# Sample tokens' gathered dots moved into the U products, and six ring slots for the V products

## The chip, the cores and the metric

The kernel runs on one core of one Trainium2 chip. The metric is the device time of one execution in microseconds (us). Five engines work side by side, each on its own instruction list: TensorE (PE, matrix products), VectorE (DVE), ScalarE (ACT), GpSimd (POOL) and SyncE (SP, which here only issues loads). They meet through semaphores.

## The reference, cut to what matters

One inference step of a hybrid decoder of two layers, for 256 prompt tokens and 32 sample tokens (8 sequences of 4), model width 1024. Each layer has a mixer and then a block of single-neuron experts (PEER), and only the latter is touched:

```python
def peer(h, wq, k1, k2, u, v):        # 16384 experts, 8 heads, top 16 each
    ...
    q = (xb @ wq).reshape(-1, PEER_HEADS, 2, half)
    s1 = jnp.einsum('thd,nd->thn', q[:, :, 0], k1)
    s2 = jnp.einsum('thd,nd->thn', q[:, :, 1], k2)
    ...                                # top 16 of 128 + 128 keys, then of their sums
    act = jax.nn.gelu(jnp.einsum('thkd,td->thk', jnp.take(u, idx, axis=0), xb).astype(jnp.float32))
    return jnp.einsum('thk,thkd->td', (gw * act).astype(xb.dtype), jnp.take(v, idx, axis=0))
```

So a token needs, for each of its 128 chosen experts, the dot product with a row of u, its GELU, a gate weight, and then the weighted sum of the rows of v.

## The kernel before

The 256 prompt tokens are computed densely: all 16384 experts, as 128 tiles of 128, each tile 128 x 1024 floats (512 KB). `experts_block` makes the **U products** (tile of u times tokens, GELU, into `m.act`), `gates_block` multiplies `m.act` by the gates of the chosen experts, and `combine_block` makes the **V products** (tile of v times `m.act`, summed over all tiles in PSUM as `ps_y`). The host lays all tiles of a layer out in the order of use in one array, `stream`; SP loads them in order into a ring of `RING` = 3 slots (`load_many`), each load waiting until the slot's tile of three before is done.

A float32 tile is multiplied in two parts. ACT copies a half tile (128 x 512) to a rounded high part (`split_high`, line 393), another engine subtracts it from the tile to make the low part (`split_low`, line 400), and PE multiplies high with high, high with low and low with high parts: 24 matmuls of 256 columns a tile (lines 443 and 447 in U, 2444 and 2448 in V). `parts` has three buffers of half a tile. The subtraction of the second half frees the ring slot (`m.done`). In U the first `TOPK_TILES` = 51 tiles have both subtractions on GpSimd, because DVE is searching the top experts; from there GpSimd has the first half and DVE the second. In V, DVE has both, and GpSimd makes the low part of the activations (line 2493, `act_parts`, once a tile). `each_tile` runs such a body over a range of tiles in loops of one **turn**, three tiles.

The 32 sample tokens are not computed densely. Their 32 x 128 choices are laid over the 128 partitions, 32 to a partition (`SLOTS` = 32), and one **gather** (an indirect DMA issued by GpSimd, line 2501) fetches one row of 1024 floats for each partition, 512 KB together, into one of the two buffers `m.rows`. All of this stands in `combine_block`: from turn `DOT` = 1, 16 turns (`HALF`) with two gathers from `u_rows` and two dot products on DVE each (`tile_dot`, line 2530: one instruction multiplies and sums a row buffer with `m.tokens`); then ACT's GELU of the 32 sums (line 2479), which waits for the last dot, and the product with the weights; then, from turn `ADD` = 18, 16 turns with two gathers of rows of v and two weighted additions into `m.tokens` each (`tile_add`, line 2542). GpSimd issues the next fetch of a buffer when DVE has counted the buffer used (`row_used0`, `row_used1`). Late in the stage PE sums the four partitions of each token (`samples_ready`, `ps_m`, line 2455).

Of the kernel before, what the change touches and what calls it, by code (L numbers as in the profile page):

```python
# [30 lines left out]
DEPTH = 2  # L31
NP = 256
# [178 lines left out]
class Memory:  # L211


    def __init__(self, nc, ctx):
# [65 lines left out]
        self.picks = t.take(NP // SPOTS * HEADS * TOPK // 2).bitcast(BF16)  # L280
        self.spots = self.rows.rearrange("p a b -> p (a b)").bitcast(BF16)
# [131 lines left out]
def each_tile(eng, first, end, body):  # L413

    assert first % RING == 0
    start, turns = first // RING, end // RING
    if turns - start == 1:
        for j in range(RING):
            body(start, j)
    elif turns > start:  # L420
        with eng.Fori(start, turns) as g:
            for j in range(RING):
                body(g, j)
    for n in range(turns * RING, end):
        body(turns, n % RING)
# [1629 lines left out]
def experts_block(nc, m, l, hr, stream, spots_in):  # L2055
# [3 lines left out]
             "picked exp_ready gates_ready turned picks_ready spots_loaded")  # L2059
    SCORES1, SCORES2, TOKENS = 2 * RING, 9 * RING, 10 * RING  # L2060
    SOFT, TURNED = TOPK_TILES + 3 * RING, TOPK_TILES + 6 * RING
    GROUPS = ((HEADS, 0, m.sel[:, :, 0, :]), (HEADS, 1, m.sel[:, :, 1, :]), (HEADS // FOLD, 0, m.sel[:, :, 2, 0:SLOTS]))
    with signals(nc, names) as s, nc.psum_tensor("ps_s", [P, 4, 512], F32) as ps_s, \
# [60 lines left out]
        def _(act):  # L2124
# [50 lines left out]
            each_tile(act, TURNED + RING, NKEYS - 2, tile)  # L2175
# [4 lines left out]
        def _(pool):  # L2180
# [6 lines left out]

            each_tile(pool, 0, TOPK_TILES, tile)
            each_tile(pool, TOPK_TILES, NKEYS, first_half)

        @block.vector
        def _(v):
# [110 lines left out]
            each_tile(v, SOFT + 2 * RING, NKEYS, second_half)  # L2303
# [99 lines left out]
def combine_block(nc, m, l, stream, u_rows):  # L2403

    AHEAD = 3
    assert RING % AHEAD == 0 and PARTS == 3
    TURNS = NKEYS // RING
    HALF = SLOTS // 2
    DOT, ADD = 1, 2 + HALF
    assert ADD + HALF <= TURNS - 3  # L2410
    names = ("step zeroed summed hi_ready lo_ready parts_used act_hi act_lo x_ready squares_ready sums_ready root_loaded "
             "root_ready row_used0 row_used1 dots_ready act_ready weighted samples_ready samples_summed")
    with signals(nc, names) as s, nc.psum_tensor("ps_y", [P, KD, NP], F32) as ps, \
            nc.psum_tensor("ps_n", [P, 512], F32) as ps_n, nc.psum_tensor("ps_m", [P, 512], F32) as ps_m, \
            nc.sbuf_tensor("act_parts", [P, AHEAD, 2, NP], F32R) as act_parts, \
            nc.sbuf_tensor("zeros", [P, 512], BF16) as zeros, \
            nc.sbuf_tensor("gated", [P, KD, NSAMP], F32) as tmp, nc.Block() as block:

        def column(g, j):
            return m.act[:, ds(g * RING + j, 1), :].squeeze(1)  # L2420
# [351 lines left out]
```

## Time and profile before

| | |
|---|---|
| median of 3 runs | 2501.21 us (2496.72 to 2512.55) |
| profiled execution | 2507.76 us, span 2506.0 us |
| PE, PEld busy | 2313.6 us (92%), 2094.0 us (84%) |
| DVE, ACT, GpSimd busy | 1556.4, 1240.3, 1081.1 us |
| DMA | 455.45 MB, mean 182 GB/s |
| granted PE clock, mean | 0.947 |

The span is the time from the first to the last instruction of the profiled execution; the rest of its time lies around it. A busy share is a mean over stages with different limits. PEld is the loading of weights, beside the matmuls. A row of a group gives the source line, engine, operation, the operands and how many; then busy time and mean time of one; then the idle time of the engine just before them and who ended it. In the view in order of time a row begins with start and duration, and ends with the idle time before it and its releaser.

### The profile page before, as it was taken

The page shows a single profiled execution, that of the slowest core. Times are in us where ns is not written, and L with a number is a line of the kernel's source. Part 1 is how long each engine was busy: PE and PEld are TensorE (multiplying, and loading weights), DVE is VectorE, ACT ScalarE, POOL GpSimd, SP SyncE. Part 2 cuts the span into 40 slices and gives each one's busy share as a digit, 9 for nine tenths or more (in the row PEclk, how much of TensorE's full clock was granted, in tenths as well). Part 3 has the DMA queues.
Part 4 walks back from the last instruction along what each step waited for, and adds up shares of the span by engine and source line. Part 5 has one row for each costly group of instructions (what it writes and reads, how often), then busy time and mean ns, then how long its engine had stood idle before and what let it go on. Part 6 is the DMA issues. An engine that isn't in the chain of part 4 may idle for free. (4 is left out here: it accounts for less than half of the span.)

```text
span 2506.0 us, 59086 instructions
## 1 busy us (share of the span) xinstructions
PE 2313.6 (92%) x20464; PEld 2094.0 (84%) x20484; DVE 1556.4 (62%) x3131; ACT 1240.3 (49%) x2355; POOL 1081.1 (43%) x1000
## 2 busy tenths in 40 slices
PE   5967999999999999999979679999999999999998
PEld 4933777999998799999969248699999988999997
DVE  3466634993224987888554766359632278888875
ACT  3530113557556955555545302145675587555554
POOL 0005202884445755555200141058744476555641
PEclk8966899999999999999989689999999999999999
DMA  6556123555553088888544560345555512888873
GB/s 263 165 176 211 53 87 126 177 179 198 186 190 111 0 270 286 280 288 279 178 147 159 185 219 3 111 160 177 184 201 188 189 43 93 281 294 273 287 244 129
DMA packets 123813, 455.45 MB, mean 182 GB/s; under 512 B 13744, under 2 KB 14256, under 8 KB 122544
## 3 DMA queue, kind: packets, MB, share of 16 engines
q1 hardware_dynamic: 105264, 386.80, 44.5%
q0 software_dynamic: 18432, 67.12, 10.0%
q8 instruction: 71, 1.16, 0.2%
q14 instruction: 46, 0.38, 0.0%
HBM read 449.37 MB, written 4.49 MB: 181 GB/s over the span
## 5 line engine op out<-in xcount | busy, mean ns | idle before, releaser
L393 ACT ACTIVATE parts<-ring 128x512 fp32r<-128x512 f32 x1128 | 698.9, 629 | 534.9 <-PE ps_u L447 281.7
L400 DVE TENSOR_TENSOR parts<-ring,parts 128x512 fp32r<-128x512 f32 x770 | 594.5, 796 | 510.3 <-ACT parts L393 488.7
L400 POOL TENSOR_TENSOR parts<-ring,parts 128x512 fp32r<-128x512 f32 x358 | 463.9, 1298 | 475.6 <-ACT parts L393 460.8
L2444 PE MATMUL ps_y<-act_parts,parts 128*128 128x256 f32 x4096 | 566.7, 280 | 11.4 <-ACT parts L393 11.0
L443 PE MATMUL ps_u<-h_parts,parts 128*128 128x256 f32 x4096 | 563.5, 280 | 0.9 <-ACT parts L393 0.6
L2444 PEld LDWEIGHTS ps_y<-act_parts,parts 128*128 128x128 f32 x4096 | 516.1, 188 | 17.3 <-ACT parts L393 16.8
L443 PEld LDWEIGHTS ps_u<-h_parts,parts 128*128 128x128 f32 x4096 | 514.9, 188 | 3.4 <-ACT parts L393 1.9
L2493 POOL TENSOR_TENSOR act_parts<-big,act_parts 128x256 fp32r<-128x256 f32 x256 | 235.8, 921 | 242.5 <-ACT act_parts L2473 239.9
L2448 PE MATMUL ps_y<-act_parts,parts 128*128 128x256 f32 x2048 | 328.9, 282 | 7.5 <-DVE parts L400 5.9
L447 PE MATMUL ps_u<-h_parts,parts 128*128 128x256 f32 x2048 | 322.3, 279 | 1.4 <-DVE parts L400 1.1
L2448 PEld LDWEIGHTS ps_y<-act_parts,parts 128*128 128x128 f32 x2048 | 275.4, 188 | 18.7 <-DVE parts L400 17.1
L447 PEld LDWEIGHTS ps_u<-h_parts,parts 128*128 128x128 f32 x2048 | 275.6, 188 | 2.2 <-DVE parts L400 1.5
L2473 ACT ACTIVATE act_parts<-big 128x256 fp32r (+1 forms) x256 | 106.7, 417 | 183.1 <-PE ps_y L2448 176.0
L2338 PEld LDWEIGHTS ps_g<-onehot 128*128 128x128 f32 x1024 | 128.4, 194 | 36.6 <-issue 31.2
L443 PE MATMUL ps_z<-x_parts,parts 128*128 128x288 f32 x832 | 132.5, 303 | 27.1 <-ACT parts L393 27.1
L2338 PE MATMUL ps_g<-onehot 128*128 128x128 f32 x1024 | 146.7, 287 | 6.5 <-ACT onehot L2370 3.4
L2358 POOL TENSOR_TENSOR onehot<-keep,sel 128x512 f32<-128x512 f32 x128 | 133.0, 1042 | 37.6 <-PE ps_g L2338 26.7
L443 PEld LDWEIGHTS ps_z<-x_parts,parts 128*128 128x128 f32 x832 | 121.0, 195 | 28.3 <-ACT parts L393 28.3
L459 PE MATMUL ps_mod<-ring,cond 128*32 128x256 f32 x768 | 78.9, 514 | 52.6 <-DMA ring<-in_stream 42.2
L2542 DVE SCALAR_TENSOR_TENSOR big<-big 128x1024 f32<-128x1024 f32 x64 | 102.5, 1602 | 29.7 <-DMA big<-in_stream,big 29.5
L2530 DVE SCALAR_TENSOR_TENSOR big<-big 128x1024 f32<-128x1024 f32 x64 | 91.7, 1432 | 39.0 <-DMA big<-in_u_rows,big 38.5
L2501 POOL DMA_INDIRECT big<-in_stream,big x64 | 76.0, 1187 | 71.9 <-DVE big L2542 68.1
(384 smaller groups left out, 2552.0 us busy)
## 6 DMA issues: line engine op xcount, KB each, us to landing
ring<-in_stream SPq DMA_DIRECT2D x696, 512.0 KB
big<-in_stream SPq DMA_DIRECT2D x16, 512.0 KB, 11.7
out_state_out<-big SPq DMA_DIRECT2D x2, 1440.0 KB, 7.0
big<-in_state SPq DMA_DIRECT2D x2, 1280.0 KB, 11.1
big<-in_mixc SPq DMA_DIRECT2D x2, 1024.0 KB, 8.5
big<-in_spots SPq DMA_DIRECT2D x2, 1024.0 KB, 5.4
x_res<-in_x SPq DMA_DIRECT2D x1, 1152.0 KB, 5.1
out_y<-big SPq DMA_DIRECT2D x4, 288.0 KB, 2.1
```

The costliest lines, as they stand in the source:

```text
L393: eng.activation(m.parts[:, q % PARTS, 0, :], half_tile(m, t, half), ACT.Copy).then_inc(s["hi_ready"], 1)
L400: eng.tensor_tensor(m.parts[:, q % PARTS, 1, :], half_tile(m, t, half), m.parts[:, q % PARTS, 0, :].bitcast(F32), ALU.subtract).then_inc(m ...
L443: pe.matmul(out, hi[:, k, :], hr[:, side, kk, 0:tokens], start=(kk + side == 0), stop=False)
L447: mm = pe.matmul(out, lo[:, k, :], hr[:, 0, kk, 0:tokens], start=False, stop=(kk == KD - 1))
L2338: mm = pe.matmul(ps_g[:, g % SETS, c, :], first[:, g % SETS, c, :], second[:, g % SETS, c, :], start=True, stop=True)
L2358: pool.tensor_tensor(second[:, g % SETS, :, :], spread(m.iota, 1, GROUP), spread(tokens_of(m.second_key, i, g), 2, P), ALU.subtract).then_ ...
L2444: pe.matmul(ps[:, half * KD // 2 + k, :], hi[:, k, :], act_parts[:, j % AHEAD, side, :], start=False, stop=False)
L2448: mm = pe.matmul(ps[:, half * KD // 2 + k, :], lo[:, k, :], act_parts[:, j % AHEAD, 0, :], start=False, stop=False)
L2473: act.activation(act_parts[:, j % AHEAD, 0, :], column(g, j), ACT.Copy).then_inc(s["act_hi"], 1)
L2493: pool.tensor_tensor(act_parts[:, j % AHEAD, 1, :], column(g, j), act_parts[:, j % AHEAD, 0, :].bitcast(F32), ALU.subtract).then_inc(s["ac ...
L2530: v.scalar_tensor_tensor(m.rows[:, q, :], m.rows[:, q, :], 1.0, m.tokens, ALU.mult, ALU.mult, accum_out=m.dot[:, ds((g - DOT) * 2 + q, 1)] ...
L2542: v.scalar_tensor_tensor(m.tokens, m.rows[:, q, :], m.dot[:, ds((g - ADD) * 2 + q, 1)], m.tokens, ALU.mult, ALU.add).then_inc(s[f"row_used ...
```

## The change

The dot products of the sample tokens move from `combine_block` to `experts_block`. There they stand in the 16 turns from `DOTS` = tile 69 to `DOTS_END` = tile 117, two gathers and two dots a turn as before, into two buffers `m.dot_rows` that lie where the activations of tiles 120 to 127 come later. GpSimd's loop is written out for these turns, and each fetch stands behind a first-half subtraction; DVE does a dot behind the second-half subtraction of the second and third tile of a turn. ACT's GELU of the sums waits at tile 120, DVE's product with the weights at tile 123.

In `combine_block` the ring has six slots (`VRING`: the three of `m.ring` and three in `more_ring`), a turn has six tiles, and the 16 turns with additions, from `ADD` = 1, have one addition behind the third and one behind the sixth tile. `act_parts` has two slots instead of three, `zeros` and `gated` move into `m.sel`, and the order of the PSUM tensors changes.

```diff
@@ Memory
+        self.dot_rows = Area(self.big, (NKEYS - 2 * D // NP) * NP).take(2, D)
@@ experts_block
+    HALF = SLOTS // 2
+    DOTS, DOTS_END = TURNED, TURNED + RING * HALF
@@ scalar
-            each_tile(act, TURNED + RING, NKEYS - 2, tile)
+            each_tile(act, TURNED + RING, DOTS_END + RING, tile)
+            act.wait_ge(s["dots_ready"], 1)
+            act.activation(m.dot, m.dot, ACT.Gelu_apprx_tanh).then_inc(s["dots_out"], 1)
+            each_tile(act, DOTS_END + RING, NKEYS - 2, tile)
@@ gpsimd
+            def fetch(n, q):
+                if n:
+                    pool.wait_ge(s[f"row_used{q}"], n)
+                pool.indirect_dma_start(m.dot_rows[:, q, :], None, u_rows,
+                                        bass.IndirectOffsetOnAxis(ap=m.u_row[:, 2 * n + q:2 * n + q + 1], axis=0)).then_inc(
+                    m.fetched[q], 16)
-            each_tile(pool, TOPK_TILES, NKEYS, first_half)
+            each_tile(pool, TOPK_TILES, DOTS - RING, first_half)
+            pool.wait_ge(s["found"], 3)
+            for turn in range(DOTS // RING - 1, DOTS_END // RING):
+                n = turn - DOTS // RING
+                for j in range(RING):
+                    first_half(turn, j)
+                    if j == 0 and n >= 0:
+                        fetch(n, 1)
+                    if j == 2 and n + 1 < HALF:
+                        fetch(n + 1, 0)
+            each_tile(pool, DOTS_END, NKEYS, first_half)
@@ vector
-            each_tile(v, SOFT + 2 * RING, NKEYS, second_half)
+            each_tile(v, SOFT + 2 * RING, DOTS, second_half)
+            def dot(g, j):
+                second_half(g, j)
+                if j:
+                    q, n = j - 1, g - DOTS // RING
+                    v.wait_ge(m.fetched[q], l * (2 * HALF * 16) + n * 16 + 16)
+                    v.scalar_tensor_tensor(m.dot_rows[:, q, :], m.dot_rows[:, q, :], 1.0, m.tokens, ALU.mult, ALU.mult,
+                                           accum_out=m.dot[:, ds(n * 2 + q, 1)]).then_inc(s[f"row_used{q}"], 1)
+            v.wait_ge(s["tokens_out"], 2)
+            each_tile(v, DOTS, DOTS_END, dot)
...
+            v.memset(m.tokens, 0.0)
+            each_tile(v, DOTS_END, DOTS_END + 2 * RING, second_half)
+            v.wait_ge(s["dots_out"], 1)
+            link(v.tensor_tensor(m.dot, m.dot, m.weight, ALU.mult))
+            each_tile(v, DOTS_END + 2 * RING, NKEYS, second_half)
@@ combine_block
-    AHEAD = 3
+    AHEAD = 2
-    TURNS = NKEYS // RING
+    TURNS = NKEYS // VRING
-    DOT, ADD = 1, 2 + HALF
+    ADD = 1
+            nc.sbuf_tensor("more_ring", [P, RING, D], F32) as more, \
+        def slot(j):
+            if j < RING:
+                n = T_V + j
+                return m.ring[:, n % RING, :], m.loaded[n % RING], m.done[n % RING], n // RING
+            return more[:, j - RING, :], s[f"loaded{j}"], s[f"done{j}"], 0
@@ sync
-            load_many(sp, m, stream, l, T_V + RING, TILES)
+            for j in range(RING, VRING):
+                tile, loaded, _, _ = slot(j)
+                sp.dma_start(tile, stream[l, T_V + j, :, :]).then_inc(loaded, 16)
+            with sp.Fori(1, TURNS) as g:
+                for j in range(VRING):
+                    load(g, j)
@@ scalar
-                act.wait_ge(s["parts_used"], g * 2 * RING + (2 * j + PARTS - 2))
+                act.wait_ge(s["parts_used"], g * 2 * VRING + (2 * j + PARTS - 2 * AHEAD + 2))
@@ gpsimd
             for turn in range(TURNS):
+                n = turn - ADD
-                for j in range(RING):
+                for j in range(VRING):
                     tile(turn, j)
+                    if j == 0 and 0 <= n < HALF:
+                        fetch(n, 1)
+                    if j == 3 and 0 <= n + 1 < HALF:
+                        fetch(n + 1, 0)
@@ vector
             def tile_add(g, j):
                 tile(g, j)
-                if j:
-                    q = j - 1
+                if j % RING == RING - 1:
+                    q, n = j // RING, g - ADD
```

## Rows read from the trace of the kernel before

**Rows 1.** The page's busy tenths, TensorE, 40 slices of 62.65 us each.

```profile
PE   5967999999999999999979679999999999999998
```

**Rows 2.** Busy time by stretch: busy and (count) per engine, clock, DMA share, GB/s.

```profile
640.00:780.00 140.00, 140.00 (x1202) 140.00 (x1201) 34.58 (x50) 76.87 (x151) 64.60 (x50) 1.00 0.58 187
883.00:1028.00 145.00, 139.10 (x1141) 134.78 (x1140) 119.57 (x157) 74.28 (x143) 84.17 (x79) 1.00 0.85 284
1038.00:1180.00 142.00, 138.44 (x1150) 135.17 (x1149) 124.87 (x125) 75.17 (x144) 80.53 (x79) 1.00 0.87 291
```

**Rows 3.** Groups of plain U products, 640 to 780 us.

```profile
L443 PE MATMUL ps_u<-h_parts,parts 128*128 128x256 f32 x802 | 109.8, 279 | 0.0
...
L400 POOL TENSOR_TENSOR parts<-ring,parts 128x512 fp32r<-128x512 f32 x50 | 64.6, 1292 | 75.4 <-ACT parts L393 75.4
...
L400 DVE TENSOR_TENSOR parts<-ring,parts 128x512 fp32r<-128x512 f32 x50 | 34.6, 692 | 105.4 <-ACT parts L393 105.4
```

**Rows 4.** Order of time in plain U products, GpSimd.

```profile
702.08 1.29 POOL L400 TENSOR_TENSOR parts<-ring,parts 128x512 fp32r<-128x512 f32 x1 [1.51 <-ACT parts L393]
```

**Rows 5.** Order of time in V, GpSimd's activation splits of tiles 3, 54, 105, both layers.

```profile
882.87 0.73 POOL L2493 TENSOR_TENSOR act_parts<-big,act_parts 128x256 fp32r<-128x256 f32 x1 [0.50 <-ACT act_parts L2473]
...
1038.42 0.74 POOL L2493 TENSOR_TENSOR act_parts<-big,act_parts 128x256 fp32r<-128x256 f32 x1 [0.68 <-ACT act_parts L2473]
...
1190.41 0.74 POOL L2493 TENSOR_TENSOR act_parts<-big,act_parts 128x256 fp32r<-128x256 f32 x1 [2.06 <-ACT act_parts L2473]
...
2114.79 0.74 POOL L2493 TENSOR_TENSOR act_parts<-big,act_parts 128x256 fp32r<-128x256 f32 x1 [0.63 <-ACT act_parts L2473]
...
2267.67 0.74 POOL L2493 TENSOR_TENSOR act_parts<-big,act_parts 128x256 fp32r<-128x256 f32 x1 [0.68 <-ACT act_parts L2473]
...
2421.19 0.74 POOL L2493 TENSOR_TENSOR act_parts<-big,act_parts 128x256 fp32r<-128x256 f32 x1 [2.09 <-ACT act_parts L2473]
```

**Rows 6.** Groups of the V stretch with dots, 883 to 1028 us.

```profile
L2444 PE MATMUL ps_y<-act_parts,parts 128*128 128x256 f32 x761 | 105.5, 280 | 4.5 <-ACT parts L393 4.4
...
L400 DVE TENSOR_TENSOR parts<-ring,parts 128x512 fp32r<-128x512 f32 x95 | 79.0, 876 | 5.4 <-ACT parts L393 5.3
L2448 PE MATMUL ps_y<-act_parts,parts 128*128 128x256 f32 x380 | 61.5, 284 | 1.4 <-DVE parts L400 1.4
L393 ACT ACTIVATE parts<-ring 128x512 fp32r<-128x512 f32 x96 | 57.7, 625 | 40.7 <-DMA ring<-in_stream 28.8 <-PE ps_y L2448 10.2 <-issue 1.5
...
L2530 DVE SCALAR_TENSOR_TENSOR big<-big 128x1024 f32<-128x1024 f32 x31 | 44.8, 1447 | 20.8 <-DMA big<-in_u_rows,big 20.6
```

**Rows 7.** Groups of the V stretch with additions, 1038 to 1180 us.

```profile
L400 DVE TENSOR_TENSOR parts<-ring,parts 128x512 fp32r<-128x512 f32 x94 | 78.3, 881 | 3.0 <-ACT parts L393 3.0
...
L393 ACT ACTIVATE parts<-ring 128x512 fp32r<-128x512 f32 x96 | 58.4, 627 | 33.8 <-DMA ring<-in_stream 18.0 <-PE ps_y L2448 12.1 <-issue 3.4
...
L2542 DVE SCALAR_TENSOR_TENSOR big<-big 128x1024 f32<-128x1024 f32 x31 | 51.4, 1659 | 14.2 <-DMA big<-in_stream,big 14.0 <-issue 0.2
```

**Rows 8.** Order of time in two turns with dots, GpSimd and DVE.

```profile
910.65 2.17 DVE L2530 SCALAR_TENSOR_TENSOR big<-big 128x1024 f32<-128x1024 f32 x1
...
913.10 1.16 POOL L2501 DMA_INDIRECT big<-in_u_rows,big  x1 [1.37 <-DVE big L2530]
...
916.27 1.66 POOL L2493 TENSOR_TENSOR act_parts<-big,act_parts 128x256 fp32r<-128x256 f32 x1 [1.24 <-ACT act_parts L2473]
...
918.07 1.23 POOL L2501 DMA_INDIRECT big<-in_u_rows,big  x1
...
919.00 1.22 DVE L2530 SCALAR_TENSOR_TENSOR big<-big 128x1024 f32<-128x1024 f32 x1
...
926.88 1.23 DVE L2530 SCALAR_TENSOR_TENSOR big<-big 128x1024 f32<-128x1024 f32 x1 [2.75 <-DMA big<-in_u_rows,big]
```

**Rows 9.** Order of time at the GELU of the dots.

```profile
1030.65 0.23 ACT L2479 ACTIVATE big<-big 128x32 f32<-128x32 f32 x1 [2.60 <-DVEq L2549]
...
1030.95 0.91 DVE L2550 MEMSET big<- 128x1024 f32 x1 [0.38 <-issue]
```

More of the change, by code:

```diff
@@ L31 @@
 DEPTH = 2
+VRING = 6
 NP = 256
@@ L410, in wait_low, with each_tile @@
         eng.wait_ge(s["lo_ready"], g * RING + (j + 1))
-def each_tile(eng, first, end, body):
-    assert first % RING == 0
-    start, turns = first // RING, end // RING
+def each_tile(eng, first, end, body, ring=RING):
+    assert first % ring == 0
+    start, turns = first // ring, end // ring
     if turns - start == 1:
-        for j in range(RING):
+        for j in range(ring):
             body(start, j)
@@ L421, in each_tile @@
         with eng.Fori(start, turns) as g:
-            for j in range(RING):
+            for j in range(ring):
                 body(g, j)
-    for n in range(turns * RING, end):
-        body(turns, n % RING)
+    for n in range(turns * ring, end):
+        body(turns, n % ring)
 def split_product(pe, m, s, first, g, j, hr, out, tokens, columns=None):
@@ new lines, in high, with low @@
+        def high(act, g, j, half):
+            tile, loaded, _, base = slot(j)
+            q = 2 * j + half
+            if half == 0:
+                act.wait_ge(loaded, g * 16 + 16 * (base + 1))
+            act.wait_ge(s["parts_used"], g * 2 * VRING + (q + 1))
+            act.activation(m.parts[:, q % PARTS, 0, :], tile[:, half * D // 2:(half + 1) * D // 2], ACT.Copy).then_inc(
+                s["hi_ready"], 1)
+        def low(v, g, j, half):
+            tile, _, done, _ = slot(j)
+            q = 2 * j + half
+            v.wait_ge(s["hi_ready"], g * 2 * VRING + (q + 1))
+            v.tensor_tensor(m.parts[:, q % PARTS, 1, :], tile[:, half * D // 2:(half + 1) * D // 2],
+                            m.parts[:, q % PARTS, 0, :].bitcast(F32), ALU.subtract).then_inc(done if half else s["lo_ready"], 1)
@@ L2425, in _, with low_is_there, bank, load @@
+        def low_is_there(pe, g, j, half):
+            _, _, done, base = slot(j)
+            if half:
+                pe.wait_ge(done, g + (base + 1))
+            else:
+                pe.wait_ge(s["lo_ready"], g * VRING + (j + 1))
+        def bank(n):
+            return ps[:, 2 * n:2 * n + 2, :]
         @block.sync
         def _(sp):
-            load_many(sp, m, stream, l, T_V + RING, TILES)
+            def load(g, j):
+                tile, loaded, done, base = slot(j)
+                sp.wait_ge(done, g + base)
+                sp.dma_start(tile, stream[l, g * VRING + (T_V + j), :, :]).then_inc(loaded, 16)
+            for j in range(RING, VRING):
[4 more added lines that the diff above has]
+                    load(g, j)
+            for j in range(NKEYS % VRING):
+                load(TURNS, j)
@@ L2457, in _ @@
             mm.then_inc(s["samples_summed"], 1)
-            each_tile(pe, RING * (TURNS - 2), NKEYS, tile)
-            for k in range(KD // 2):
-                pe.matmul(pair(k), zeros[:, 0:P], zeros[:, :], start=False, stop=True).then_inc(s["summed"], 1)
+            each_tile(pe, VRING * (TURNS - 2), NKEYS, tile, VRING)
+            for n in range(4):
+                pe.matmul(bank(n), zeros[:, 0:P], zeros[:, :], start=False, stop=True).then_inc(s["summed"], 1)
             for k in range(KD):
```

115 lines of the change are left out of this document (48 added, 67 removed).

## The prediction

> **What bounds the kernel now.** I read the 40 slices of the page first, then busy time by stage, then the groups of the stages that the change touches, last the order of time inside them. TensorE is busy in 92% of the span and stands at nines in nearly every slice of both expert stages of each layer (the U products, then, behind two slices of gates, the V products) [rows 1]. Where nothing is added to them, both stages are TensorE's alone: the DVE splits of plain U products leave the matmuls 0.0 us of idle time [rows 3], and one tile starts every 2.80 us, in U (GpSimd's split of 1.29 us and the 1.51 us idle before it [rows 4]) and in V alike (0.74 and 2.06 us at 1190.41 [rows 5]). A turn of three tiles is 8.40 us. That is the floor, and the change has no fewer matmuls, so it can only give back what the V stage takes above it.
>
> How much is that? The GpSimd split of the activation comes once a tile, so its starts are a clock [rows 5]. Layer 0: from tile 3 (882.87) to tile 54 (1038.42), the 17 turns with the dots and the GELU of the dots, 155.55 us against 17 x 8.40 = 142.80, so 12.75 too many. From there to tile 105 (1190.41), the 17 turns with the weighted additions, 151.99, so 9.19 too many. Layer 1: 2114.79, 2267.67 and 2421.19 give 152.88 (10.08 too many) and 153.52 (10.72). So **dots 12.75 + 10.08 = 22.83 us, additions 9.19 + 10.72 = 19.91 us, together 42.7 us**. After tile 105 of layer 0 the starts are 2.80 us apart again. The sample sums on TensorE, once a layer behind that, stay as they are.
>
> Who takes it? In the 145 us of dots, DVE is busy 119.6 us [rows 2], waits 20.6 us for gathered rows and 5.3 us for ACT [rows 6]: 145.5 us. DVE has nothing left there. While it waits for a gather, the low parts and the release of ring slots queue behind it; ACT then waits 28.8 us for ring tiles [rows 6]. The additions read the same: DVE busy 124.9 of 142 us [rows 2], 14.0 us of waiting for gathers and 18.0 us of ACT waiting for the ring [rows 7]. The DMA side is loaded too: 284 and 291 GB/s in the two stretches against 187 in plain U [rows 2]. Three tiles and two gathers of 512 KB each are 5 x 0.524 MB = 2.62 MB a turn; at the floor of 8.40 us that would be 312 GB/s, and no stretch of [rows 2] shows it.
>
> **The change, part by part.**
>
> *Additions in V.* The additions go from two every three tiles to one. Six tiles now have 12 splits and 2 additions on DVE: at the crowded 0.881 and 1.659 us [rows 7] that is 10.6 + 3.3 = 13.9 of 16.8 us, where before it was 2 x (5.3 + 3.3) = 17.2 us, more than the floor. The traffic falls to 4 x 0.524 MB in 8.40 us = 250 GB/s, under the 284 that is reached today. The ring is six slots instead of three, so a slot has 8.4 us more to come back in, against ACT's waits of 18.0 us over some 16 turns, 1.1 us a turn [rows 7]. A fetch is issued five tiles (14 us) before its use, where a slow gather takes 8.8 us from issue to use [rows 8]. The additions last from tile 6 to tile 101, within the stage. I take 0.5 us a layer as what is left of their loss, bounds 0 and 9.19 (nothing gained): -19.9 + 1 = **-18.9 us**. With two activation slots in place of three nothing moves: ACT's condition for writing one evaluates to the same count as before (2j + 1 in both).
>
> *Dots out of V.* **-22.8 us.** With them goes a stop: the GELU of the dots on ACT waits 2.60 us for DVE [rows 9]. In U ACT's wait comes three tiles after the last dot, DVE's wait for the result three tiles later still, and it takes 0.23 us [rows 9] of an ACT that is busy 76.9 of 140 us [rows 2]. The memset (0.91 us [rows 9]) and the multiplication go to a DVE that is idle 105 of 140 us [rows 2]: nothing.
>
> *Dots into U, 16 turns a layer.* Each turn they bring two GpSimd issues of 1.16 to 1.23 us [rows 8], two DVE products of 1.45 us [rows 6] and the same 2.62 MB. On DVE: 3 splits x 0.69 [rows 3] + 2 x 1.45 = 5.0 of 8.40 us. In V it was 6 x 0.876 + 2.9 = 8.2 [rows 6]. So 3.4 us a turn are free in U, where V's dots waited 20.6 us over 145/9.15 = 16 turns (155.55/17 = 9.15), 1.3 us a turn, for gathers. A DVE instruction queued behind the wait is one second-half split, not two. This cover hides DVE's part; without it the stage would lose the 22.8 us again. On GpSimd: 3 splits x 1.29 [rows 3] + 2 x 1.2 = 6.3 of 8.40 us; the idle piece before each split is 1.51 us [rows 4] and an issue fits into it, barely. On the ring: it keeps three slots, and nothing relieves it but that DVE frees them in time. This is where I expect the loss: ACT waited 28.8 us for tiles in V's dots, 1.8 us a turn, and TensorE's own idle time for ACT and DVE in that stretch was 4.5 + 1.4 us on the matmuls [rows 6]. I take half of V's 0.71 us a turn (22.83/32), 0.35 us, since one of its two causes (the full DVE) is gone and the other (2.62 MB a turn through three slots) is not: 32 x 0.35 = **+11.2 us**. Bounds: 0 (plain U never waits) and 22.8 (as in V); the value is my choice between them. The GpSimd waits are on products that DVE has started early, so what queues behind them (the next first-half split) has the 1.51 us.
>
> *A shared resource.* The rows show it: GpSimd's activation split takes 0.74 us alone [rows 5] and 1.66 us when it meets a DVE product, and a DVE product takes 1.22 us or, with GpSimd at work as it starts, 2.17 us [rows 8]. In U the GpSimd splits are longer, so more of them meet. If all three stretch by the 0.92 us seen, GpSimd needs 3 x 2.21 + 2 x 1.23 = 9.1 us a turn and becomes the bound: +0.7 us x 32 = 22.3 us, all that the dots gave back in V. The Trainium skill speaks against the change here: "SBUF — State Buffer", section "Who interferes with whom", says that a DVE instruction with two SBUF inputs contends with a GpSimd instruction that reads SBUF, and that whichever was issued first makes the other wait. By that rule the trace agrees (0.74 against 1.66). It is the second route of rival A, and 0.07 of A's chance.
>
> *Loads, loops, order of banks.* Three more tile loads are issued at the start of V, when the queue is idle: nothing. Loop bodies of six tiles instead of three, the GpSimd code of U written out, other PSUM banks: nothing in plain stretches hangs on them; 0, at most 1 us a layer either way.
>
> **Sum**, against the profiled execution's own 2507.8 us: -18.9 - 22.8 + 11.2 = -30.5, giving 2477.3. The profiled execution is 6.6 us above the median of the three runs (2501.2), so the median should go to 2501.2 - 30.5 = **2471 us** (1.2% faster).
>
> **Rivals.**
> A. *The dots cost in U what they cost in V* (the traffic of 2.62 MB a turn through three slots is the whole cause, or GpSimd becomes the bound). For it: 284 and 291 GB/s and ACT's waits for the ring. Against it: DVE's 145.5 of 145 us. Then only the additions gain: 2501.2 - 18.9 = 2482.
> B. *Nothing of the dots is lost in U.* For it: plain U has 0.0 us of idle matmul time, and 3.4 us of DVE and 2.1 us of GpSimd free each turn. Then -41.7: 2459.5.
> C. *Slower: the gather's round trip in U.* A row buffer is refilled by a GpSimd that first does the next tile's first-half split. If each time the product (2.17), the stretched split (2.21) and a slow gather (8.8 from issue to use [rows 8]) follow one another, a buffer comes back after 13.2 us, not 8.40: +4.8 x 32 = 153 us, less the 41.7, gives 2613. It decides from a turn of 8.40 + 41.7/32 = 9.70 us; over that the kernel is slower than before. Against it: gathers of about 6 us stand beside the slow ones (913.10 to 919.00 in [rows 8]), and the split can be done while the gather is still under way.
> D. *The additions keep their loss* although thinned, because gathers disturb ring loads at any rate: 2501.2 - 22.8 + 11.2 = 2490. Against it: 250 GB/s and six slots.
>
> **How the numbers follow.** Forecast (a turn of U between 8.45 and 8.9 us) 0.50, A 0.22, B 0.15, C 0.06, D 0.07. The range of 8 in 10 runs from B's 2459.5, less 3.5 us for the spread of a median, to above A and D: 2456 to 2491. Over and under 1% (25 us) is about what a measurement of this kernel can tell from no change. Faster by over 1% means below 2476: all of B and 0.45 of the forecast's 0.50 (its upper end is 32 x 0.5 = 16 us lost, 2476), so 0.60. Within 1%: the rest of the forecast, A, D, and a little of C, 0.35. Slower by over 1%: 0.05.
>
> **What would show it.** In the profile after: starts of the activation split in V 2.80 us apart but for the sample sums, from tile 6 to 101 too; no gather that DVE waits for in V, and no ring wait on ACT. In U, from tile 69 to 117, GpSimd's first-half splits 8.40 us apart each third if B, 8.75 if I am right, 9.1 if A. Of A's two routes, GpSimd busy near 9 us a turn shows the second; ACT waiting for ring tiles the first. I am wrong if the dots in U show DVE waiting for gathers with second-half splits late behind it, or if V's turns of six stay above 17 us.

## The result, and the profile after

| | before | after |
|---|---|---|
| median | 2502.85 us (2496.72 to 2512.55, 8 runs) | 2491.48 us (2486.21 to 2493.31, 8 runs) |
| profiled execution | 2507.76 us, span 2506.0 | 2486.21 us, span 2484.4 |
| DVE, ACT, GpSimd busy | 1556.4, 1240.3, 1081.1 us | 1523.3, 1234.5, 1073.5 us |
| granted PE clock, mean | 0.947 | 0.947 |

The ratio is 0.9949, with a 95% interval of 0.993 to 0.9968. The same kernel, run again later beside before, gave 0.9973 (0.9944 to 1.0001). So the change is worth between nothing and 0.7%, where 1.2% was forecast. The profiled execution is the lowest of its eight, so what follows says where time went inside one execution, and the ratios say how much it was.

**V.** The same clock as [rows 5], GpSimd's split of the activation, tiles 3, 54 and 105 of layer 0 and then of layer 1, in order of time:

```profile
895.90 0.74 POOL L2582 TENSOR_TENSOR act_parts<-big,act_parts 128x256 fp32r<-128x256 f32 x1 [2.06 <-ACT act_parts L2565]
...
1038.70 1.16 POOL L2582 TENSOR_TENSOR act_parts<-big,act_parts 128x256 fp32r<-128x256 f32 x1 [2.06 <-ACT act_parts L2565]
...
1181.50 0.74 POOL L2582 TENSOR_TENSOR act_parts<-big,act_parts 128x256 fp32r<-128x256 f32 x1 [2.06 <-ACT act_parts L2565]
...
2114.62 0.74 POOL L2582 TENSOR_TENSOR act_parts<-big,act_parts 128x256 fp32r<-128x256 f32 x1 [2.06 <-ACT act_parts L2565]
...
2257.41 1.16 POOL L2582 TENSOR_TENSOR act_parts<-big,act_parts 128x256 fp32r<-128x256 f32 x1 [2.06 <-ACT act_parts L2565]
...
2400.22 0.74 POOL L2582 TENSOR_TENSOR act_parts<-big,act_parts 128x256 fp32r<-128x256 f32 x1 [2.06 <-ACT act_parts L2565]
```

Every step of 51 tiles takes 142.8 us, 2.80 us a tile; nothing is left of the 42.7 us that [rows 5] gave. The whole stage, first to last such split, went from 377.82 to 357.32 us in layer 0 and from 378.61 to 355.88 in layer 1: 43.2 us less. Busy time by stretch: first U with dots and V with additions of layer 0, then the same of layer 1 (columns as in [rows 2]):

```profile
626.00:771.00 145.00, 139.00 (x1131) 133.91 (x1131) 76.15 (x111) 71.07 (x147) 101.54 (x78) 1.00 0.82 276
895.00:1180.00 285.00, 285.00 (x2445) 285.00 (x2444) 198.46 (x236) 160.39 (x306) 127.78 (x134) 1.00 0.74 246
1848.00:1992.00 144.00, 139.05 (x1126) 134.41 (x1125) 72.39 (x111) 70.49 (x146) 102.76 (x77) 0.99 0.83 277
2115.00:2400.00 285.00, 285.00 (x2445) 285.00 (x2444) 198.87 (x236) 159.94 (x306) 127.41 (x134) 1.00 0.75 247
```

TensorE is busy in all of V, with DVE at 198 of 285 us. In U it is idle for 6 of 145 and 5 of 144 us, where plain U had none [rows 2], and in these idle pieces, and in matmuls that take longer beside them, the gain goes back. Groups of layer 1's V: ACT waits for nothing but TensorE there, and for no ring tile:

```profile
L2484 ACT ACTIVATE parts<-ring 128x512 fp32r<-128x512 f32 x102 | 63.8, 625 | 18.3 <-PE ps_y L2540 18.3
L2484 ACT ACTIVATE parts<-more_ring 128x512 fp32r<-128x512 f32 x102 | 63.6, 624 | 18.3 <-PE ps_y L2540 18.3
```

**U.** The clock here is ACT's GELU, once a tile. Tiles 51 and 127 of layer 0, then of layer 1, before:

```profile
576.56 0.39 ACT L2135 ACTIVATE big<-ps_u 128x256 f32 x1
...
788.17 0.38 ACT L2135 ACTIVATE big<-ps_u 128x256 f32<-128x256 f32 x1 [2.42 <-PE ps_u L447]
...
1806.80 0.39 ACT L2135 ACTIVATE big<-ps_u 128x256 f32 x1
...
2018.44 0.38 ACT L2135 ACTIVATE big<-ps_u 128x256 f32<-128x256 f32 x1 [2.41 <-PE ps_u L447]
```

and after:

```profile
573.31 0.38 ACT L2140 ACTIVATE big<-ps_u 128x256 f32 x1
...
798.48 0.38 ACT L2140 ACTIVATE big<-ps_u 128x256 f32<-128x256 f32 x1 [2.42 <-PE ps_u L449]
...
1794.89 0.38 ACT L2140 ACTIVATE big<-ps_u 128x256 f32 x1
...
2019.79 0.38 ACT L2140 ACTIVATE big<-ps_u 128x256 f32<-128x256 f32 x1 [2.41 <-PE ps_u L449]
```

76 tiles of 2.80 us are 212.8 us. Before: 211.61 and 211.64, an **excess** of -1.2 us a layer. After: 225.17 and 224.90, an excess of +12.4 and +12.1. So U lost 13.56 + 13.26 = **26.8 us** in this execution, where 11.2 were forecast. With V's -43.2 that makes -16.4; the gates between the stages take 1.2 us more, and the other 6.4 us of the 21.6 by which the span fell lie in stages that the change doesn't touch. (In the later profile of the same kernel the excess was 9.1 and 5.3: the loss in U differs from execution to execution.) Most of it lies in the turns with dots: of the 26.8 us, 23.1 come between tiles 72 and 117, and 3.7 before tile 72.

Groups of the U stretch of layer 0, as those of [rows 3] and [rows 6]:

```profile
L445 PE MATMUL ps_u<-h_parts,parts 128*128 128x256 f32 x755 | 104.6, 280 | 2.6 <-ACT parts L395 2.5
...
L402 POOL TENSOR_TENSOR parts<-ring,parts 128x512 fp32r<-128x512 f32 x48 | 73.0, 1521 | 35.8 <-ACT parts L395 35.2
L449 PE MATMUL ps_u<-h_parts,parts 128*128 128x256 f32 x376 | 61.3, 285 | 3.4 <-POOL parts L402 2.9
L395 ACT ACTIVATE parts<-ring 128x512 fp32r<-128x512 f32 x96 | 60.0, 629 | 73.9 <-DMA ring<-in_stream 43.5 <-PE ps_u L449 30.3
...
L2336 DVE SCALAR_TENSOR_TENSOR big<-big 128x1024 f32<-128x1024 f32 x31 | 42.2, 1360 | 7.2 <-DMA big<-in_u_rows,big 7.2
L402 DVE TENSOR_TENSOR parts<-ring,parts 128x512 fp32r<-128x512 f32 x48 | 35.2, 734 | 62.7 <-POOL parts L402 57.9 <-ACT parts L395 4.8
L2200 POOL DMA_INDIRECT big<-in_u_rows,big x30 | 29.4, 979 | 9.3 <-DVE big L2336 5.5 <-issue 1.4
```

DVE waits less for gathers (7.2 us against 20.6 in [rows 6]). It waits for GpSimd, 57.9 us, which was not what ended its waits in plain U [rows 3]. GpSimd's split has grown from 1292 to 1521 ns. Which of two meeting instructions gets longer is decided by their order. In the turns with dots of both layers, the 55 DVE products inside which a GpSimd split starts take 1.21 to 1.23 us, and the 4 products that start inside a split take 2.32; the 54 splits that start inside a product take 1.71 us on average (up to 2.32), and the 36 that meet no DVE instruction 1.30. And ACT waits 43.5 us for ring tiles, more than V's dots cost it before (28.8 [rows 6]). One slot in order of time shows how these hang together; first ACT, then GpSimd, then DVE:

```profile
696.88 0.63 ACT L395 ACTIVATE parts<-ring 128x512 fp32r<-128x512 f32 x1 [1.76 <-DMA ring<-in_stream]
...
705.63 0.64 ACT L395 ACTIVATE parts<-ring 128x512 fp32r<-128x512 f32 x1 [1.81 <-DMA ring<-in_stream]
```

```profile
691.62 2.04 POOL L402 TENSOR_TENSOR parts<-ring,parts 128x512 fp32r<-128x512 f32 x1
...
697.60 1.59 POOL L402 TENSOR_TENSOR parts<-ring,parts 128x512 fp32r<-128x512 f32 x1 [1.51 <-ACT parts L395]
```

```profile
699.31 0.75 DVE L402 TENSOR_TENSOR parts<-ring,parts 128x512 fp32r<-128x512 f32 x1 [1.27 <-POOL parts L402]
```

A tile is there at 696.88. ACT's first half is followed by GpSimd's split, 1.59 us; DVE's second half waits for it and frees the slot at 700.06; the next tile is in the slot 5.57 us later, at 705.63, three tiles on. That is 8.75 us for what has to take 8.40, and ACT waits. So a slot's turn contains GpSimd's split. While ACT waits for the ring, what makes that split longer (the one at 691.62 starts inside a DVE product and takes 2.04 us) or starts it later (an issue ahead of it) makes the next tile later. The refill is the other part: a ring load takes a median of 4.7 us from issue to landing in this stretch.

### The profile page after: what moved, and what is told of

Same layout as the page of the kernel before. It is cut to its first block and busy times, and to the rows that moved or that the text cites. A ratio compares the mean times of both kernels' runs of the same rounds, so it can differ in the third digit from the quotient of the medians.

```text
span 2484.4 us, 58392 instructions
## 1 busy us (share of the span) xinstructions
PE 2305.5 (93%) x20464; PEld 2091.6 (84%) x20484; DVE 1523.3 (61%) x3131; ACT 1234.5 (50%) x2355; POOL 1073.5 (43%) x1000
## 3 DMA queue, kind: packets, MB, share of 16 engines
q0 software_dynamic: 18432, 67.12, 10.4%
## 5 line engine op out<-in xcount | busy, mean ns | idle before, releaser
L402 POOL TENSOR_TENSOR parts<-ring,parts 128x512 fp32r<-128x512 f32 x358 | 488.4, 1367 | 399.9 <-ACT parts L395 383.7
L395 ACT ACTIVATE parts<-ring 128x512 fp32r<-128x512 f32 x616 | 385.9, 631 | 387.0 <-PE ps_u L449 219.1
L2536 PE MATMUL ps_y<-act_parts,parts 128*128 128x256 f32 x4096 | 562.0, 280 | 0.0
L2582 POOL TENSOR_TENSOR act_parts<-big,act_parts 128x256 fp32r<-128x256 f32 x256 | 216.3, 845 | 422.6 <-ACT act_parts L2565 422.6
L402 DVE TENSOR_TENSOR parts<-ring,parts 128x512 fp32r<-128x512 f32 x258 | 184.8, 718 | 339.2 <-ACT parts L395 196.3
L2540 PE MATMUL ps_y<-act_parts,parts 128*128 128x256 f32 x2048 | 321.6, 279 | 0.0
L449 PEld LDWEIGHTS ps_u<-h_parts,parts 128*128 128x128 f32 x2048 | 276.2, 189 | 16.7 <-POOL parts L402 14.4
L2491 DVE TENSOR_TENSOR parts<-ring,parts 128x512 fp32r<-128x512 f32 x260 | 205.1, 800 | 123.3 <-ACT parts L2484 122.6
L2491 DVE TENSOR_TENSOR parts<-more_ring,parts 128x512 fp32r<-128x512 f32 x252 | 199.6, 802 | 117.4 <-ACT parts L2484 117.4
L2484 ACT ACTIVATE parts<-ring 128x512 fp32r<-128x512 f32 x260 | 162.3, 625 | 51.5 <-PE ps_y L2540 51.5
L2484 ACT ACTIVATE parts<-more_ring 128x512 fp32r<-128x512 f32 x252 | 157.2, 624 | 45.2 <-PE ps_y L2540 45.2
## 6 DMA issues: line engine op xcount, KB each, us to landing
big<-in_state SPq DMA_DIRECT2D x2, 1280.0 KB, 11.2
```

Of the source, the lines that this page charges most:

```text
L395: eng.activation(m.parts[:, q % PARTS, 0, :], half_tile(m, t, half), ACT.Copy).then_inc(s["hi_ready"], 1)
L402: eng.tensor_tensor(m.parts[:, q % PARTS, 1, :], half_tile(m, t, half), m.parts[:, q % PARTS, 0, :].bitcast(F32), ALU.subtract).then_inc(m ...
L449: mm = pe.matmul(out, lo[:, k, :], hr[:, 0, kk, 0:tokens], start=False, stop=(kk == KD - 1))
L2484: act.activation(m.parts[:, q % PARTS, 0, :], tile[:, half * D // 2:(half + 1) * D // 2], ACT.Copy).then_inc(s["hi_ready"], 1)
L2491: v.tensor_tensor(m.parts[:, q % PARTS, 1, :], tile[:, half * D // 2:(half + 1) * D // 2], m.parts[:, q % PARTS, 0, :].bitcast(F32), ALU.s ...
L2536: pe.matmul(ps[:, half * KD // 2 + k, :], hi[:, k, :], act_parts[:, j % AHEAD, side, :], start=False, stop=False)
```

## The experiments

All start from the changed kernel unless said. The table has the excess in U as above, tiles 51 to 127, of the profiled execution; the change itself is there three times (the V-only experiment has its U code unaltered). The loss against before is the excess plus 1.2 us a layer. Gathers of 32 KB, no product and one dot a turn leave out part of the work, so they only locate the loss.

| kernel | us (runs) | ratio to before | excess in U, layers 0, 1 |
|---|---|---|---|
| change | 2491.48 (8) | 0.9949 (0.993 to 0.9968) | 12.4, 12.1 |
| change again | 2486.61 (10) | 0.9973 (0.9944 to 1.0001) | 9.1, 5.3 |
| V loads three ahead | 2481.43 (1) | | 6.0, 12.1 |
| gathers of 32 KB | 2470.81 (1) | | 1.0, 3.6 |
| no product on DVE | 2482.11 (1) | | 6.5, 6.2 |
| one dot a turn | 2476.36 (1) | | 3.6, 1.1 |
| six slots in U | 2479.73 (5) | 0.9899 (0.9863 to 0.9936) | 6.0, 6.4 |
| DVE both halves | 2466.61 (1) | | 4.2, 1.8 |
| DVE both, six slots | 2474.01 (6) | 0.9916 (0.9885 to 0.9947) | 3.3, 4.9 |
| change, one table | 2479.57 (8) | 0.9942 (0.9922 to 0.9962) | 5.5, 7.3 |
| DVE both, one table | 2465.85 (5) | 0.9869 (0.9842 to 0.9897) | 2.2, 0.2 |
| DVE both, six slots, one table | 2474.61 (6) | 0.991 (0.9878 to 0.9942) | 5.8, 2.2 |
| before, six slots in V | 2496.98 (10) | 1.0008 (0.9983 to 1.0032) | -1.5, -0.3 |

Before's own medians beside these were 2503.59, 2494.51 and 2494.06 us on three chips, which is why times are compared by ratio. Over its three profiles the change's excess is 9.5 us a layer on average (5.3 to 12.4), and its loss over both layers 26.8, 16.7 and 20.5 us. So a single layer at 6, or a loss near 16, says little.

### What in U costs: bytes, product, list

**Gathers of 32 KB** leave GpSimd's list and DVE's products as they are and take away nearly all of the gathers' bytes. (A memset of the row buffers, 1.81 us on GpSimd, stands once a layer ahead of the turns.)

```diff
-                pool.indirect_dma_start(m.dot_rows[:, q, :], None, u_rows,
+                pool.indirect_dma_start(m.dot_rows[:, q, 0:64], None, u_rows.rearrange("r (a b) -> (r a) b", b=64),
```

> Measured by the starts of the GELU, the U stage from tile 51 to tile 127 takes 13.6 us (layer 0) and 13.3 us (layer 1) longer in the changed kernel than before, 26.8 us together; this is the loss to be explained. Here each gather fetches 64 floats a partition (32 KB) in place of 1024 (512 KB); the GpSimd issues, the DVE products over the full buffers and all waits stay. The sample tokens' dots are not the reference's. If the loss is traffic (five 512 KB transfers a turn on three ring slots): it falls to under 4 us together, ACT's 90 us of waiting for ring tiles in the two dot stretches nearly goes. If it is the engines (GpSimd splits stretched to 1.52 us by DVE products, the chain GpSimd, DVE, slot release): 18 us or more stay. If it is the gathers' round trip: it falls as well, but then e4 keeps its loss.

**No product on DVE** keeps bytes and issues.

```diff
-                    v.scalar_tensor_tensor(m.dot_rows[:, q, :], m.dot_rows[:, q, :], 1.0, m.tokens, ALU.mult, ALU.mult,
-                                           accum_out=m.dot[:, ds(n * 2 + q, 1)]).then_inc(s[f"row_used{q}"], 1)
+                    v.sem_inc(s[f"row_used{q}"], 1)
```

> DVE waits for each gathered row buffer and marks it used, but makes no product; gathers of full size, GpSimd issues and waits stay. The sample tokens' dots are left out (zero). If the loss is traffic: 20 us or more of the 26.8 us stay, with GpSimd's splits back at 1.3 us. If it is the engines' contention: it falls under 8 us.

Groups of U, 640 to 755 us, with small gathers:

```profile
L402 POOL TENSOR_TENSOR parts<-ring,parts 128x512 fp32r<-128x512 f32 x41 | 57.8, 1410 | 11.6 <-ACT parts L395 11.0
L395 ACT ACTIVATE parts<-ring 128x512 fp32r<-128x512 f32 x82 | 51.9, 633 | 52.8 <-PE ps_u L449 42.1 <-issue 7.4 <-DMA ring<-in_stream 3.2
...
L2338 DVE SCALAR_TENSOR_TENSOR big<-big 128x1024 f32<-128x1024 f32 x28 | 48.8, 1742 | 0.0
```

and without the product:

```profile
L402 POOL TENSOR_TENSOR parts<-ring,parts 128x512 fp32r<-128x512 f32 x39 | 50.8, 1302 | 37.1 <-ACT parts L395 36.5 <-issue 0.2
...
L395 ACT ACTIVATE parts<-ring 128x512 fp32r<-128x512 f32 x78 | 48.5, 629 | 59.6 <-DMA ring<-in_stream 41.8 <-PE ps_u L449 17.2 <-issue 0.5
```

Without the bytes the ring waits are gone (3.2 us) and most of the loss with them, though GpSimd and DVE still hold each other up (1410 and 1742 ns). A loss of 6.9 us stays, more than the 4 expected of traffic alone and far from the 18 expected of the engines. Without the product the split is back (1302 ns, plain U's 1292 [rows 3]) and the ring waits stay (41.8 us); its loss of 15.0 us lies between the two expectations, below the change's mean and hardly under its lowest profile. So the traffic is a cause without which little is lost, and the product's share can't be told from the spread.

**One dot a turn** halves gathers and products. It loses 7.1 us in both layers together, a little over the 6 expected. But 6.8 of them come before tile 72: in the 15 turns from there to tile 117 it loses 0.2 us in layer 0 and nothing in layer 1. Busy time from 640 to 755 us:

```profile
640.00:755.00 115.00, 115.00 (x979) 115.00 (x978) 44.80 (x69) 62.11 (x122) 68.51 (x54) 1.00 0.72 252
```

TensorE is busy throughout, and a ring load takes a median of 3.7 us to land where it took 4.7 in the change. So three slots with GpSimd's split in their turn are enough for four transfers and one product a turn, and in the change not for five and two.

```diff
-                    if j == 0 and n >= 0:
-                        fetch(n, 1)
...
-                if j:
+                if j == 1:
```

> The changed kernel with one gather and one dot a turn in U in place of two; the other 16 dots of each layer are left out (zero). Ring of three slots and GpSimd's first-half splits as in the change. Four 512 KB transfers a turn, as in the V stage. If three slots are enough for four transfers: the loss of 26.8 us falls under 6 us. If the order GpSimd, DVE, release is too slow for any gather beside it: over 10 us stay.

### Six slots in U

Tiles 72 to 107 get three further slots, laid where activations come later. It should end the ring waits and leave GpSimd's list.

```diff
+U_FIRST, U_LAST = 72, 108
+        self.more_u = Area(self.big, U_LAST * NP).take(RING, D)
...
+            load_many(sp, m, stream, l, T_U + SOFT, T_U + U_FIRST)
+            for n in range(U_FIRST, NKEYS + RING):
+                tile, loaded, done, before = place(n)
+                if before:
+                    sp.wait_ge(done, before)
+                sp.dma_start(tile, stream[l, T_U + n, :, :]).then_inc(loaded, 16)
```

> The changed kernel with three more ring slots in U for tiles 72 to 107 (they lie where the activations of tiles 108 to 119 come later), 12 of the 16 dot turns; all else, traffic and engines, as in the change. A correct kernel. If the cause is the cycle of three slots with loads lengthened by the gathers: the 12 turns go back to 8.40 to 8.45 us, the loss falls from 26.8 to some 5 to 8 us, and the kernel takes about 2472 us against 2491. If DMA bandwidth is the limit (312 GB/s would be needed): the turns stay near 9.2 us and the time near 2491. If the gathers' round trip or the engines are: the same, near 2491.

The ring waits are gone, and the turns settle at 8.73 to 8.76 us, not at the 8.40 to 8.45 expected; 14.7 us of loss stay where 5 to 8 were expected. Order of time, GpSimd, one turn:

```profile
701.39 3.18 POOL L2094 TENSOR_TENSOR parts<-ring,parts 128x512 fp32r<-128x512 f32 x2
705.93 1.16 POOL L2282 DMA_INDIRECT big<-in_u_rows,big  x1 [1.36 <-DVE big L2426]
707.12 1.44 POOL L2094 TENSOR_TENSOR parts<-big,parts 128x512 fp32r<-128x512 f32 x1
708.71 1.41 POOL L2282 DMA_INDIRECT big<-in_u_rows,big  x1
710.13 3.17 POOL L2094 TENSOR_TENSOR parts<-big,parts 128x512 fp32r<-128x512 f32 x2
```

and DVE beside it:

```profile
703.33 2.32 DVE L2426 SCALAR_TENSOR_TENSOR big<-big 128x1024 f32<-128x1024 f32 x1
...
706.19 1.21 DVE L2426 SCALAR_TENSOR_TENSOR big<-big 128x1024 f32<-128x1024 f32 x1
```

From 701.39 to 710.13 GpSimd has two splits (3.18 with the gap between them), a wait of 1.36 for a DVE product, an issue 1.16, a split 1.44, an issue 1.41, and 0.19 of gaps. That is 8.74 us. The product it waits for (703.33) starts inside GpSimd's second split and takes 2.32 us instead of 1.21. So behind the ring stands a second bound, at 0.34 us a turn: GpSimd's list together with the DVE product in its way.

### DVE makes both low parts in the turns with dots

GpSimd then only gathers; no split of its own stands in a slot's turn.

```diff
+                    if n < 0:
-                    first_half(turn, j)
+                        first_half(turn, j)
...
             def dot(g, j):
-                second_half(g, j)
+                split_low(v, m, s, T_U, g, j, 0)
+                split_low(v, m, s, T_U, g, j, 1)
...
+            pool.wait_ge(s["lo_ready"], DOTS_END)
             each_tile(pool, DOTS_END, NKEYS, first_half)
```

> In the 16 dot turns DVE makes both low parts of a tile, and GpSimd only issues the gathers. The slot release no longer waits for GpSimd's split of 1.52 us, and nothing meets on the shared port but the issues. DVE then has 6 splits and 2 products a turn, about 7 us of 8.4. If the chain over GpSimd in the slot's cycle is the main part: the loss falls from 26.8 to about 10 us. If it is DMA traffic alone: it stays within 4 us of 26.8. If a full DVE is what cost in V: it rises.

Groups of U, 640 to 755 us:

```profile
L402 DVE TENSOR_TENSOR parts<-ring,parts 128x512 fp32r<-128x512 f32 x79 | 52.9, 690 | 14.9 <-ACT parts L395 14.1
...
L395 ACT ACTIVATE parts<-ring 128x512 fp32r<-128x512 f32 x80 | 50.0, 630 | 57.0 <-DMA ring<-in_stream 39.0 <-PE ps_u L449 16.4 <-issue 1.3
...
L2339 DVE SCALAR_TENSOR_TENSOR big<-big 128x1024 f32<-128x1024 f32 x27 | 33.0, 1222 | 17.4 <-DMA big<-in_u_rows,big 17.0 <-issue 0.2
```

Both operations are back at their unstretched 690 and 1222 ns. ACT still waits for the ring (39.0 us), yet the loss is small: a tile that comes late has its first half subtracted in 0.69 us rather than 1.3 to 2.0, and TensorE is idle 1.5 us of the 115. The loss is 8.3 us, near the 10 expected. DVE now waits for gathers, 17.0 us. Two things go at once here, GpSimd's place in the slot's turn and the meetings of its splits with products; that without the product alone 15.0 us stay speaks for the place, by one profile of each.

**Both together** (six slots and DVE's splits):

> e3 and e4 together: in the dot turns DVE makes both low parts and GpSimd only issues gathers, and tiles 72 to 107 of U have six ring slots. A correct kernel. e3 left 8.3 us of the 26.8 us (the ring still late), e4 left 14.7 us (turns of 8.74 us, GpSimd's list full). If those are the only two limits: the loss falls under 3 us, the turns between tile 75 and 107 are 8.40 to 8.45 us, and the kernel takes about 2466 us. If there is a third (DMA bandwidth at 312 GB/s, the gathers' round trip, a full DVE at 6 splits and 2 products): turns of 8.6 us or more remain and it takes 2472 us or more.

It lost 10.5 us against before in U, not under 3. A miss: DVE waits for gathers as much with six slots (16.8 us, 640 to 740) as with three, so what is left is not the ring. What it is was not taken apart; two row buffers and their round trip are the candidate, by argument only.

### Table loads

In the profile after, ACT loads two activation tables in every turn from tile 51 to 71, in order of time:

```profile
613.15 1.28 ACT L395 ACT_TABLE_LOAD   x1
614.44 0.63 ACT L395 ACTIVATE parts<-ring 128x512 fp32r<-128x512 f32 x1
615.10 1.28 ACT L2140 ACT_TABLE_LOAD   x1
```

They stand in before as well, where TensorE is busy 62.3 of the 63 us from 577 to 640. The loop is entered behind an Exp. A GELU of one column ahead of the loop removes them:

```diff
             act.activation(m.sel[:, 2, 2, 0:SLOTS], m.sel[:, 2, 2, 0:SLOTS], ACT.Exp).then_inc(s["exp_ready"], 1)
+            act.activation(m.rms[:, NT - 1:NT], m.eps, ACT.Gelu_apprx_tanh)
```

> In both kernels ACT loads two activation tables (2 x 1.28 us) in every turn of U between tiles 51 and 71, because the loop there is entered behind an Exp; two of these turns are the first with gathers in the changed kernel. Here the changed kernel has one GELU of a single column behind the Exp, so the loop is entered with its own table. If these loads delay the slots where the gathers begin: the turns from tile 63 to 71 fall from 9.5 to 10.1 us to 8.4 to 9.0, and the loss in U falls by 2 to 5 us over both layers. If they are hidden: no turn moves but by chance.

> e3 (DVE makes both low parts in the dot turns) with e10's single GELU: a correct kernel on the ring of three slots. e3 took 2466.6 us in one run with 8.3 us of loss left, 3 to 4 of it in the turns from tile 63 to 71. Expected 2463 to 2468 us; if the table loads are hidden, as e3.

> e5 (both low parts on DVE and six slots in U) with e10's single GELU. If late slots are what e3 has left, this beats e11 by 2 to 4 us; if e11's remaining loss is DVE waiting for gathers (21.1 us of such waits in e5), the two are alike, since six ring slots do nothing for the two row buffers.

The turn at tile 63 fell from 8.6 to 9.8 us to 8.40 in all three. On the change alone that is all: its turns at tile 66 take 8.85 and 10.92 us, its loss before tile 72 is 4.1 us (2.6 to 6.0 in the change's three profiles), and the ratio (0.9942) is not apart from the two of the change. With DVE's splits the loss before tile 72 is 0.6 and 0.7 us, against 1.9 and 3.4 without the GELU. That gave the best kernel here, **0.9869 (0.9842 to 0.9897)**, 1.3% faster than before and clear of every interval of the change. Six slots on top gained nothing: 0.991, a median 8.8 us higher and a loss in U of 10.4 us against 4.8, where equal or 2 to 4 us better was expected. How much of 0.9869 is the table's isn't settled: DVE's splits alone have a single run, 2466.61, which is 0.985 of before's median on its chip.

In that best kernel, layer 1 ran from 1897 to 1964 us with all five transfers a turn, on three slots, at turns of 8.40 us:

```profile
1897.00:1964.00 67.00, 67.00 (x577) 67.00 (x576) 49.95 (x81) 36.61 (x73) 18.35 (x16) 1.00 0.90 315
```

So 315 GB/s are moved there with TensorE never idle, and DMA bandwidth was not the limit of these turns.

### The V side: thinning or slots?

**V loads three ahead**: additions thinned as in the change, but SP issues a load only when the slot of three tiles before is free, so six slots serve as three.

```diff
-                sp.wait_ge(done, g + base)
+                _, _, near, near_base = slot((j + RING) % VRING)
+                sp.wait_ge(near, g + (near_base + (j >= RING)))
```

> The changed kernel, but in V a load also waits until the tile three before it is done, so that only three tiles are ahead as with three slots; the additions stay at one every three tiles. If the thinned additions alone cured V: its turns stay at 8.40 us. If the six slots were needed: 5 us or more a layer come back, with ACT waiting for tiles. I expect under 2 us a layer: four transfers a turn, 250 GB/s, leave room.

**Before, with six slots in V**: `experts_block` and the dense dots and additions of before, on the change's ring of six.

> The kernel before with six ring slots and turns of six tiles in V, and nothing else of the change: dots and additions both in V, two every three tiles, U plain. A correct kernel. If three slots with late tiles were V's loss: most of the 42.7 us goes, V's turns are 8.4 to 8.6 us, and the kernel takes about 2466 to 2472 us, less than the changed kernel. If DVE with its full list was the cause (my account in the prediction): at least half the loss stays, 2480 us or more.

The excess of V over 127 tiles of 2.80 us was 22.2 and 23.0 us before, 1.7 and 0.3 after. With thinning but three ahead it is 3.2 and 1.8, within the 0.3 to 4.8 that the kernels with the change's V code show, so the thinner traffic (one addition every three tiles, no dots) did it and not the slots, as expected. With six slots but dense it is 17.6 and 15.6: over half of the loss stays, as expected of the account in the prediction, and the time doesn't move (1.0008, 0.9983 to 1.0032). Groups of the latter's V with dots, 883 to 1028 us:

```profile
L2498 PE MATMUL ps_y<-act_parts,parts 128*128 128x256 f32 x392 | 63.2, 283 | 5.2 <-DVE parts L2449 5.2
...
L2582 DVE SCALAR_TENSOR_TENSOR big<-big 128x1024 f32<-128x1024 f32 x31 | 43.9, 1416 | 18.7 <-DMA big<-in_u_rows,big 18.5
```

The ring waits are gone, and TensorE waits for DVE instead. So by these profiles the late ring was about a quarter of V's loss (12.0 of 45.2 us), and what holds the rest is DVE's list, of work and of waits for gathers (18.5 us here). These two were not separated by a run. One comparison speaks for the work: the best kernel above has the same six subtractions, two products and five transfers a turn in U and no loss from 1897 to 1964 us, but there they take 0.69 and 1.22 us and not 0.86 and 1.42, and DVE waits 0.5 us for gathers.

**The change again**, as a control for all of these:

> The changed kernel, unaltered, beside the next three, for its time on the same chip and for how far the loss in U moves from one profile to the next: 12.4 and 12.1 us of excess between tiles 51 and 127 in the first profile, but 6.0 and 12.1 in e6, whose U stage is the same. Expected near 2491 us, V's turns at 8.40 us, U's excess between 6 and 13 us a layer.

It took 2486.61 us with V's turns at 8.40; its excess in U was 9.1 and 5.3 us, the second just under the range.

## Why the prediction was wrong

**Right: additions in V, -18.9, and dots out of V, -22.8.** Together -41.7; measured -43.2, and the 1 us set aside for a rest wasn't needed between tiles 3 and 105. The reading behind it (DVE 145.5 of 145 us, waits for gathers included) held against slots alone. So did the quiet end of the dots: nothing waits at tiles 120 and 123.

**Wrong: dots into U, +11.2.** It came to +26.8 in the profile after, above the upper bound of 22.8, and by all three profiles to 2 x (9.5 + 1.2) = 21 us. By its own sign, 8.75 us a turn if right and 9.1 if A, the turns from tile 69 to 117 took 9.04 and 9.03 us in the profile after, and 8.63 to 8.90 in the two later ones. Three sentences of that step failed.

*"One of its two causes (the full DVE) is gone"*, hence half of V's loss. DVE had room indeed (76 of 145 us), but in U the release of a ring slot stands behind GpSimd's first half, which in V it did not: there DVE has both halves. The relief on one list was paid on another that is in series with the ring. DVE waited 57.9 us for GpSimd, and taking GpSimd out of that path (and its meetings with products with it) brought the mean excess from 9.5 us a layer to 3.5 without the GELU ahead of the loop (two kernels), and from 6.4 to 2.6 with it. The other cause, which the step did keep, stands in series with it, and curing either cures most: without the gathers' bytes 6.9 of the 26.8 us were left, with DVE's splits 8.3.

*"3 splits x 1.29 + 2 x 1.2 = 6.3 of 8.40 us"*. The step priced GpSimd alone, and wrote the stretching beside it as a case of small chance. It is the usual case here: 1521 ns a split, and a product of 2.32 us for which the next issue waits. The list with that wait is at 8.74 us when the ring is out of the way. By the Trainium skill, "SBUF — State Buffer", section "Who interferes with whom", this had to be expected for each pair that meets; the trace agrees (1302 ns with no product, 1521 with it), and also on which of the two waits: the one that starts second (1.22 us for a product that came first, 2.32 for one that came second).

*"22.8 (as in V)" as an upper bound*. A bound from another stage holds only if the moved work meets the same lists there.

Of rival A's two routes, both are there in one kernel: the ring (8.75 us for the slot's turn shown) first, GpSimd with its wait (8.74 us) right behind it, so that curing one shows the other. A priced them as either, and the whole at no more than V's loss. Its 2482 is nearer to the measured 2491.48 than the forecast's 2471. D's 2490 is nearest of all, but by luck: it has the additions keep their loss in V, and they kept none. Rival C's mechanism (the gather's round trip) showed only as the 7.2 us of DVE's waiting.

**Not accounted for.** The profiles give -43.2 + 21 + 1 = -21 us; the ratios give -13 (0.9949) and -7 (0.9973). There is one profile of before, and V's excess in other executions of it isn't known: in the kernel with six slots alone the profile showed 12 us less in V, and the time none. Part of before's 45 us may belong to that execution. Stretches that hold none of the moved work vary as well: from the last activation split of layer 0 to the first GELU of layer 1 the fourteen profiles took 399.2 to 412.8 us (402.2 before, 399.2 after; 410.8 at a granted clock of 0.83 with six slots, DVE's splits and one table, where before had 0.86).

## What to carry to other kernels

When work is moved beside another loop, write down for each shared buffer the chain from "filled" to "free", with every engine in it, and price that chain with the durations stretched by the moved work, not each engine's list alone. Where two engines hold each other up, give the pair to one of them, if its list has room: here DVE did in 0.69 us the subtraction that took GpSimd 1.52. Waits of the same kind (here ACT's for the ring) can follow from another engine's full list in one stage and set the pace in the next. Before weighing an edit by one profile, see how far stretches move that the edit doesn't touch.

## What was not expected of the hardware

- When a DVE product (two inputs, with sum) and a GpSimd split meet, the one that starts second takes longer: the product 2.32 us instead of 1.21, the split 1.71 on average instead of 1.30. The one that starts first keeps its time if it is the product (1.21 to 1.23 us in 55 meetings).
- One core moved 303 GB/s over 115 us with DVE's splits, 307 in the best kernel, and there 315 over 67 us of layer 1 at turns of 8.40 us. That no stretch of before showed 312 GB/s was no sign of a limit.
- ACT reloads two tables of 1.28 us each turn when a loop with Copy and GELU is entered behind an Exp; one instruction ahead of the loop stopped it.
- The same code gave an excess between 5.3 and 12.4 us in one stage of one layer, so one profile can't weigh an edit that is worth less than this difference.
